# The modulation product in four-slab batches of 512 columns, or in 128-column pieces placed singly between dense slabs

## The reference

```python
def first_block(x, ...):
    for l in range(DEPTH):
        h = rms_norm(x, norm_mix_pre[l])
        mix = hybrid_mixer(h, ...)
        x = x + rms_norm(mix, norm_mix_post[l])
        h = rms_norm(x, norm_ffn_pre[l])
        x = x + rms_norm(swiglu(h, w_ffn_in[l], w_ffn_out[l]), norm_ffn_post[l])
    return x

def adaln(cvec, w, b, n):
    m = jax.nn.silu(cvec) @ w[:, : n * D_MODEL] + b[: n * D_MODEL]
    return jnp.split(m, n, axis=-1)
```

## Time and profile before

| | |
|---|---|
| median of 3 runs | 2503.66 us (2502.77 to 2505.79) |
| the profiled execution's own time | 2500.43 us |
| its span | 2498.8 us |
| mean granted clock of TensorE | 0.94 |
| PE busy | 2247.9 us, 90% |
| DVE busy | 1425.2 us, 57% |
| ACT busy | 1044.5 us, 42% |
| POOL busy | 303.8 us, 12% |
| transfers | 349 MB, 140 GB/s in the mean |

### The profile page before, as it was taken

How to read it: one execution, slowest core, us unless ns; L and a number is a source line. 1 busy time by engine, 2 the same in 40 slices (tenths; PEclk the granted TensorE clock), 3 DMA queues, 4 the chain that set the end, 5 groups by cost and what they waited for, 6 DMA issues and landing times. The chain is left out here.

```text
span 2498.8 us, 29164 instructions
## 1 busy us (share of the span) xinstructions
PE 2247.9 (90%) x11116; PEld 1796.6 (72%) x11116; DVE 1425.2 (57%) x2187; ACT 1044.5 (42%) x1664; POOL 303.8 (12%) x310
## 2 busy tenths in 40 slices
PE   8999898898999998979997877889989898887999
PEld 6777676787777776768876664667767787656997
DVE  5665574454465647545445886554444325966774
ACT  4545554443444455534443434322222223543443
POOL 0017120000000532210000540000000000600000
PEclk9999999999999999989998988889999998987999
DMA  7644335565555433466564213423333435333554
GB/s 227 185 124 127 105 115 160 181 177 183 191 175 157 141 102 95 138 201 180 160 205 159 63 51 93 135 93 110 101 101 110 135 101 168 94 119 117 162 183 161
DMA packets 184121, 349.15 MB, mean 140 GB/s; under 512 B 11824, under 2 KB 23216, under 8 KB 183984
## 3 DMA queue, kind: packets, MB, share of 16 engines
q1 hardware_dynamic: 183984, 347.29, 44.4%
HBM read 346.19 MB, written 1.05 MB: 139 GB/s over the span
## 5 line engine op out<-in xcount | busy, mean ns | idle before, releaser
L816 DVE TENSOR_TENSOR wlo<-wraw,whi 128x1024 fp32r<-128x1024 f32 (+1 forms) x538 | 646.2, 1207 | 682.0 <-ACT whi L1009 678.7
L1009 ACT ACTIVATE whi<-wraw 128x1024 fp32r<-128x1024 f32 (+1 forms) x552 | 562.7, 1027 | 648.0 <-PE psum L1770 546.3
L1770 PE MATMUL psum<-whi,act_h 128*128 128x512 f32 (+2 forms) x1424 | 578.4, 406 | 31.8 <-DVE p L1320 22.1
L1770 PE MATMUL psum<-wlo,act_h 128*128 128x512 f32 (+2 forms) x1424 | 564.7, 397 | 0.0
L1770 PE MATMUL psum<-whi,act_l 128*128 128x512 f32 (+2 forms) x1424 | 563.8, 396 | 0.0
L1770 PEld LDWEIGHTS psum<-whi,act_h 128*128 128x128 f32 x1424 | 277.1, 195 | 105.6 <-DVE p L1320 24.7
L1770 PEld LDWEIGHTS psum<-whi,act_l 128*128 128x128 f32 x1424 | 275.7, 194 | 62.2
L1770 PEld LDWEIGHTS psum<-wlo,act_h 128*128 128x128 f32 x1424 | 276.6, 194 | 56.5
L1770 PE MATMUL psum<-act_h,whi 128*128 128x512 f32 (+1 forms) x704 | 244.0, 347 | 23.7 <-DVE wlo L816 19.8
L1770 PE MATMUL psum<-act_l,whi 128*128 128x512 f32 (+1 forms) x704 | 242.2, 344 | 0.0
L1770 PE MATMUL psum<-act_h,wlo 128*128 128x512 f32 (+1 forms) x704 | 242.2, 344 | 0.0
(11 more groups left out here) (270 smaller groups left out, 2693.4 us busy)
## 6 DMA issues: line engine op xcount, KB each, us to landing
wraw<-in_w_in SPq DMA_DIRECT2D x136, 512.0 KB, 3.7
wraw<-in_w_gate SPq DMA_DIRECT2D x104, 512.0 KB, 3.7
wraw<-in_w_mod SPq DMA_DIRECT2D x96, 512.0 KB, 3.7
wraw<-in_w_ffn_in SPq DMA_DIRECT2D x80, 512.0 KB, 3.7
wraw<-in_w_ffn_out SPq DMA_DIRECT2D x44, 512.0 KB, 4.2
wraw<-in_w_down SPq DMA_DIRECT2D x44, 512.0 KB, 4.3
wraw<-in_w_val SPq DMA_DIRECT2D x40, 512.0 KB, 4.6
wraw<-in_w_branch SPq DMA_DIRECT2D x32, 512.0 KB, 3.9
```

The source lines that it names most:

```text
L816: eng.tensor_tensor(wlo[:, i, 0:st.n, 0:st.w], wraw[:, st.s % RING_W, 0:st.n, 0:st.w], whi[:, i, 0:st.n, 0:st.w].bitcast(F32), ALU.subtrac ...
L1009: nc.scalar.activation(whi[:, d % RING_S, 0:st.n, 0:st.w], wraw[:, s % RING_W, 0:st.n, 0:st.w], ACT.Copy).then_inc(sem("slab_rounded"), 1)
L1770: return nc.tensor.matmul(out, lhsT, rhs, start=start, stop=stop)
```

## The change

1. The modulation product is cut into 96 pieces of 128 columns, 48 a layer, each of full depth: one transfer of 512 KB from a weight array that the host has laid out by pieces, and 8 matmuls of 128 columns in four column groups. A piece is placed behind a dense slab (`st.after`), a ride: in block 1 behind every fifth from the thirteenth on (64 rides), in block 2 in each layer 8 in w_in_2 (behind every second slab) and 8 in FFN_2 (every fifth). Ahead of each ride stands the reader of the piece before.
2. Reader and ride share one bank, 3 in block 1 and 7 in block 2. Dense chunks then turn through banks 0 to 2 in block 1, and 0 to 6 in FFN_2; the misc banks of block 2 are 4 to 6.
3. The batches and their readers go from w_out, norms, w_ffn_out, ysplit, FFN_2 and attention.
4. All tiles of p are evacuated by ACT.
5. The attention loop is written t(i-2), s(i), m(i-1), v(i-2).
6. Two pads shift the tiles so that `act_h` to `y_l`, `hid_h`, `hid_l`, `act2_h` and `act2_l` lie 256 B (mod 512) from the rings, as `hid2_h` and `hid2_l` still do.
7. The condition's step goes to the tenth slab of block 1.

```diff
+OPERAND_AT, OPERAND_STEP = 384, 512
...
-        self.turns = (0, 1, 2, 3)
+        self.turns = (0, 1, 2)
...
+        self.mod_queue, self.mod_every, self.mod_since, self.mod_bank = [], 5, -8, 3
...
+            pl.mod_since += 1
+            if pl.mod_queue and pl.mod_since >= pl.mod_every:
+                pl.mod_since = 0
+                st.after = mod_ride(pl)
...
+def mod_ride(pl):
+    l, c = pl.mod_queue.pop(0)
+    steps = mod_reader(pl)
+    n = len(pl.mod_reads)
+    st = Step(kind="slab", s=len(pl.slabs), weight="w_mod_2", layer=l, c=c, evac="mod", mc=n, banks=[pl.bank(pl.mod_bank)],
+              first=True, last=True, war=pl.mod_reads[n - 2] if n >= 2 else [])
...
+    return steps + [st]
...
+    pl.free, pl.mod_bank, pl.turns = (4, 5, 6), 7, (0, 1, 2, 3)
...
+        pl.mod_queue, pl.mod_every, pl.mod_since = [(l, c) for c in MOD_GATES[0]], 2, -4
...
-            for kind, u in (("att2_m", i - 1), ("att2_t", i - 2), ("att2_s", i), ("att2_v", i - 2)):
+            for kind, u in (("att2_t", i - 2), ("att2_s", i), ("att2_m", i - 1), ("att2_v", i - 2)):
...
+        pl.mod_queue, pl.mod_every, pl.mod_since = [(l, c) for c in MOD_GATES[1]], 5, 0
...
-        pl.turns = tuple(range(8))
+        pl.turns = tuple(range(7))
...
+    pl.steps = [one for st in pl.steps for one in [st] + st.after]
...
+        def at_offset(name, stack):
+            n = (OPERAND_AT - nc.sbuf_base) % OPERAND_STEP
+            if n:
+                sb(name, [P, n // 4], F32, stack)
...
-                        for t in range(0, st.tiles, 2):
+                        for t in range(st.tiles):
...
-                    if st.evac == "p":
-                        for t in range(1, st.tiles, 2):
-                            filled(dve, st.banks[t])
-                            dve.tensor_copy(p[:, t, st.col:st.col + st.w], psum[:, st.banks[t][0], 0:st.w]
-                                            ).then_inc(free(st.banks[t]), 1)
...
+                    w = wraw[:, st.s % RING_W, :, :].rearrange("p k n -> p (k n)")
+                    for k in range(KD):
+                        r = 32 * (k % 4)
+                        ins = dot(psum[r:r + 32, bk[0], 0:P], condm[:, k, :], w[:, k * P:(k + 1) * P], k < 4, k >= 4)
```

More of the change, by code:

```diff
@@ L174, in gemm @@
             pl.slabs.append(st)
-            if evac != "mod":
-                st.d = len(pl.dense)
-                pl.dense.append(st)
+            st.d = len(pl.dense)
+            pl.dense.append(st)
             steps.append(st)
-    return steps
[L182 to L192, removed]
@@ new lines, in mod_reader @@
+def mod_reader(pl):
+    st, pl.mod_last = pl.mod_last, None
+    if st is None:
+        return []
+    l, c, part = st.layer, st.c, st.c // KD
+    bk = pl.bank(pl.mod_bank)
+    pl.mod_reads.append([(f"psum_full{bk[0]}", bk[1] + 1)])
+    if part in (2, 5):
+        return [Step(kind="mod_gate", l=l, c=c, mc=st.mc, gate=part // 3, j=c % KD, waits=drained(*st.banks), banks=[bk])]
+    steps = [Step(kind="mod_cols", l=l, c=c, mc=st.mc, waits=drained(*st.banks), banks=[bk])]
+    if part in (1, 4) and c % KD == KD - 1:
+        steps.append(Step(kind="mod_gain", l=l, i=part // 3, waits=drained(bk)))
@@ L209, in mod_reader @@
     return steps
 def plan_first(pl):
-    filler = list(MOD_COLS)
+    pl.mod_queue = [(i, c) for i in range(DEPTH) for c in MOD_COLS]
     for l in range(DEPTH):
@@ L268, in plan_first @@
                (36, Step(kind="decay_turn", **decay)), (37, cb)]
+        if l == 0:
+            ssm.append((10, Step(kind="cond")))
         ybanks = [pl.bank(6), pl.bank(7)]
@@ L509, in plan_second @@
         att += pending
-        stream = []
         agate = Step(kind="agate", l=l, tiles=T, n=aln[0].n, banks=[pl.gemm_bank(), pl.gemm_bank()])
[L513 to L528, removed]
+        cback = Step(kind="cback", l=l, tiles=T, banks=[pl.gemm_bank() for i in range(T // 2)])
+        cln = ln(C_C, 2, drained(*cback.banks))
+        stream = [agate, cback, cln[0], cln[1], Step(kind="csilu", l=l, tiles=T, n=cln[0].n)]
         pl.steps += interleave(stream, att)
         pl.turns = (0, 1, 2, 3)
-        mods = fill()
-        pl.steps += mods
         order = [0, 1, 6, 7, 2, 3, 4, 5]
@@ L566, in plan_second @@
             pl.tick("hid_lo", w // P)
[L567 to L574, removed]
+        assert not pl.mod_queue
+        pl.steps += mod_reader(pl)
         pl.turns = (0, 1, 2, 3)
@@ L895, in _ @@
                     need(sp, [was.used if was.evac == "mod" else was.split])
+                if st.evac == "mod":
+                    sp.dma_start(wraw[:, st.s % RING_W, :, :].rearrange("p k n -> p (k n)"), A["w_mod_pieces"][st.layer, st.c]
+                                 ).then_inc(sem(f"slab_landed{st.s % RING_W}"), 16)
+                    continue
                 w = A[st.weight]
@@ L2041, in constants @@
     cs2 = np.stack([np.cos(ang2), np.sin(ang2)], 1).reshape(2, P, 64).transpose(1, 0, 2).reshape(P, 128)
-    rows = np.zeros((P, 4))
-    for half in range(2):
-        for s in range(2):
-            rows[[32 * half + s, 64 + 32 * half + s], 2 * half + s] = 1
+    rows = np.zeros((P, 2))
+    for j in range(4):
+        rows[[32 * j, 32 * j + 1], [0, 1]] = 1
     return np.concatenate([eye, upto, np.ones((P, P)), later, zero, later, later.T, zero, later.T, cs, neg, cs2, rows],
```

114 lines of the change are left out of this document (47 added, 67 removed).

## The result

The changed kernel takes 2617.99 us (median of 4 runs, 2613.22 to 2622.40) against 2504.72 for the kernel before measured with it: a ratio of 1.045, 95% interval 1.0425 to 1.0476. It is slower by 113 us. Slower was forecast, 2544 us in the likeliest case and at most 2600; the time lies outside the range. Of the times further down, that of v4_before_pads_ring5 is the median of three runs: its fourth (2553.3 us at a granted clock of 0.84, where the three have 0.95) was a slow run.

What follows compares the result with a forecast made beforehand. The prediction took PE's matmuls plus PE's pauses to bound the kernel. From 2500.4 us, -174 removed, +120 for rides and +94 for new waits gave 2540.4, with 3.2 to the median 2544 us; range 2445 to 2600.

Steps and rivals of the forecast that it cites:

- What was removed: Batches in block 1, block 2 and FFN_2, slabs in attention, and slower operand addresses: together -174 us.
- A single ride: Reader, DVE's add and 8 matmuls: 1.3 us each in block 1, 1.8 for gate pieces in FFN_2; all 96 +120.
- a sign of being wrong: The forecast is wrong if PE waits under 0.5 us for DVE's modT before rides.
- The chain behind a ride: After a ride at R: refill R + 0.7, rounding ends R + 5.9, low half R + 7.2; PE needs the bank R + 4.8.
- The addresses: Activation tiles moved to 256 B from the weight rings: 6.5 ns less per 512-column matmul, -38 us.
- rival B: The addresses do nothing, the 226 ns being another property of w_down; the rest as forecast, 2582 us; chance 0.09.
- The 16 in w_in_2: Rides in block 2's w_in_2, where PE waits for DVE anyway: half a microsecond each, +8 us.
- I count two thirds: New waits behind rides, 141 us in all, overlap because ACT and DVE catch up in each stall: +94 us.
- the whole list: New waits at most: 65 us at block 1 chunk ends, 32 for late adds, 44 for other items; in all 141.
- p on ACT: p all evacuated by ACT in front of the rounding, with attention's start: 12 us of new waits at most.
- half clock: PE running at half clock after the longer of the new stalls: 20 us at most.
- rival A: ACT and DVE catch up in idle time and the gaps win: faster, 2485 or 2450 us; chance 0.40.

Runs made afterwards that it cites:

- v4_before_pads_ring5: The kernel before with the two pads and five ring slots in place of four; 2443.6 us.
- e1_pads: The kernel before with nothing but the two pads; 2485.4 us against 2508.0, ratio 0.990.

## Why the prediction was wrong, step by step

**Right.** That PE's own work plus its pauses set the time, and the direction, which had been given only a little over even odds (0.53). *What was removed*: 165 of 174 us; with 23 to 28 for the addresses the batches and attention come to 137 to 142, against 136. The parts fit less well: block 1's seven gaps shrank by 44 us and not 52, FFN_2 of layer 0 by 62 with the addresses, where 50 and some 6 had been taken, and attention lost 11 and 7 us against e1_pads (from the last dense matmul before it to the first behind, in layer 0 with one batch at ysplit), where 7.5 and 11.5 had been taken. That the sum is so close is partly luck. *A single ride*: 1.26 us against 1.3 and, for gate pieces, 2.08 - 0.23 = 1.85 against 1.8, though by other parts, and the closeness is luck: the turnaround is 0.68 and not 0.8, the ride 0.57 to the next matmul and not 0.4, and the 0.1 for entry doesn't show behind a reader. The 0.4 rested on a misreading: the eight records of the earlier trace rows are four matmuls of 256 columns, a slab's 1024 in all, and a ride's 8 matmuls of 128 are the same 1024, so there was nothing to be halved. PE's idle time ahead of an undisturbed ride is 0.40 us, under the 0.5 that the prediction named as a sign of being wrong; over all 63 it is 1.05 in the mean. *The chain behind a ride*: each step within 0.5 us, and the feed-forward input product of layer 0, the stage for which the prediction named a time, took 148 us from its first dense matmul to its last (508.16 to 656.60), against 147. *The addresses* (rival B falls): by the Trainium skill's rule that weight loading doesn't take read bandwidth from the running matmul (TensorE: Matmul & The Clock Gate, Step-by-step: what each phase is for) no placement would matter; 0.226 and 0.234 changed places with the operand's address in e1_pads, so there is an effect here that the rule doesn't cover. Its size on the path was 23, and with hid2 left in place perhaps 28 (an estimate), not 38.

**Wrong: "The 16 in w_in_2 lie where PE waits for DVE anyway; half a microsecond each, +8".** The two stages cost 21 and 22 us over the kernel without rides. The row that I read the earlier trace rows says that PE waited for DVE 22.4 us in all, in 7 places. That PE already waits for an engine doesn't hide a new wait for it: DVE works there in stretches of up to 9.88 us, and each addition is one more appointment with it, at a place where PE otherwise had slabs in hand (0, 6.5, 0.7, 3.5, 6.4, 0.7, 10.6 and 0.7 us idle ahead of the eight rides of layer 0). Undisturbed they would have been 1.85 each, 30 in all, and even that was not hidden.

**Wrong: "They overlap, because in each stall ACT and DVE catch up; I count two thirds: +94".** Of the 275 us 140 are undisturbed rides (64 x 1.26 + 32 x 1.85), so the new waits came to 135, nearly the 141 of the whole list. By stage they are 90 in block 1 (the list has 65 + 18 there), 31 in the two FFN_2 (14 + 12), 13 in w_in_2 (nothing), and none for p on ACT (12), with the list's 20 for half clock spread over them; so the total fits the list in part by luck, but block 1 alone shows that no third was saved by overlap. 41 us of block 1's 90 are adds that came late (18 in the list): PE stood that much longer at its 63 readers than the undisturbed 0.68 us. The half clock was taken too low as well, if anything: it held 342 us of the change's span and 241 without rides (mean granted clock 0.935 and 0.949), which would be up to 50 us lost (an estimate) if PE worked through all of it. The argument of catching up failed because DVE and ACT could not catch up: in the rows above they are idle, 4.77 and 3.69 us, waiting for the same landing. Catching up is what an engine with work in hand does. That was said against rival A in the prediction itself (a landing that no idle time brings forward) and not applied to the forecast.

The sum closes: 22 us for w_in_2 beyond its 8 (30 undisturbed), 41 for the waits, 9 for smaller gains, chiefly the addresses, together 72; 2618 - 2544 is 74.

**What was never asked** is why the ring had four slots. The term "a ride takes a ring slot and gives it back only when used" named the cause, and its cure, one number, was worth 84 us in the change and 33 before it. The rule of the Trainium skill weighed in the prediction (TensorEngine Tiling (Array Packing), Key Properties: a change of tiling mode drains the TensorE) stays a small matter: a lone visit with nothing to wait for (readers ahead) is 0.89 us from matmul to matmul, 0.66 more than none, and with five slots 64 of them in block 1 cost 82 us with all that follows.

Not tried: whether ride and reader in banks of their own would take the last turnarounds in w_in_2. Open: why w_in of block 1 gained less from the addresses than its matmuls, and why attention got 3 to 4 us shorter in each layer with the pads alone and with the ring alone. A fourth dense bank beside the rides was not run either, so what the third bank adds once a slab is late is not known.

## What to carry to other kernels

Work that is taken in small pieces between other work pays its hand-overs once per piece: look at the bank, the ring slot and the in-order queue that each piece passes through, and give its consumer a slab's time before the next piece needs the same bank. A slot that is released by use and not by copy stops everything in order behind the next refill; one more slot is the first thing to try. And an engine that others wait for in a stage is the last place to add a hand-over to, even a short one.

## What the runs showed of the hardware

- Matmuls of 512 fp32r columns start 226 to 227 ns apart when the activation tile lies a multiple of 256 B from the weight rings (0 and 256 seen), 233 to 234 at 224 and 288 B, and 232 to 234 at 384 B (w_in and w_out of block 1 232 in the mean, the ten steps of the earlier trace rows 234), at full clock (2.4 GHz).
- With 256 columns it is the other way round, by less: in FFN_2 of layer 1 (activations stationary) 12 steps take 1.41 us in the kernel before, at 224 B, and 1.44 us in e1_pads, at 256 B:

```profile
2330.06 0.28 PE L1770 MATMUL psum<-act_h,wlo 128*128 128x256 f32 x1
...
2331.47 0.28 PE L1770 MATMUL psum<-act_h,wlo 128*128 128x256 f32 x1
```

```profile
2309.78 0.28 PE L1780 MATMUL psum<-act_h,wlo 128*128 128x256 f32 x1
...
2311.22 0.28 PE L1780 MATMUL psum<-act_h,wlo 128*128 128x256 f32 x1
```

- With a 32-wide float32 stationary operand, eight matmuls of 128 columns last 0.57 us to the next full-width matmul (484.25 - 483.68 above), and four of 256 columns the same 0.57, 0.48 within a batch (1.93 / 4): the same number of columns costs the same, cut either way, and a visit by itself adds some 0.1 us at its entry and 0.1 at its end.
